# GpSimd's first loads behind the first modulation pieces, and the second round's down matrices ahead of the ranking wait

## The reference

```python
mod = silu(c) @ w_ada[l] + b_ada[l]          # six vectors of 1024: shift1, scale1, gate1, shift2, scale2, gate2
h = x * (1 + scale1) + shift1
y = token_mixer(h, ...)                      # h @ w_in, attention, spatial gating, branches, w_out
x = layer_norm(ALPHA * x + gate1 * y, ...)
h = x * (1 + scale2) + shift2
y = moe_ffn(h, ...)                          # sigmoid scores, top 4 of 8 groups, top 8 of 64 experts, and a shared expert
x = layer_norm(ALPHA * x + gate2 * y, ...)
```

## Time and profile before

| | us |
|---|---|
| three runs | 3248.99, 3258.33, 3268.69 |
| median of the runs | 3258.33 |
| span of the profiled execution | 3257.8 |
| TensorE busy in it | 3010.5 (92%) |
| VectorE busy in it | 1343.3 (41%) |
| layer 0: start and mixer, up to the router | 0 to about 271 |
| layer 0: expert stage | about 271 to 771 |
| layer 1: expert stage | about 1014 to 1516 |

### The profile page before, as it was taken

One profiled execution on the slowest core, in us unless ns is written; L12 is line 12 of the kernel. 1 busy time (PEld: TensorE's weight loads), 2 busy tenths in 40 slices (PEclk: granted clock), 3 DMA queues, 4 the chain that ended last, 5 costly groups with the idle time before them and its releaser, 6 DMA issues.

```text
span 3257.8 us, 65550 instructions
## 1 busy us (share of the span) xinstructions
PE 3010.5 (92%) x28216; PEld 2277.8 (70%) x28216; DVE 1343.3 (41%) x2300; ACT 648.5 (20%) x1253; POOL 173.2 (5%) x160
## 2 busy tenths in 40 slices
PE   7999999888999998887999999999998989998999
PEld 6877555455877665555867744488878877896888
DVE  6645332225545332224553256353057255555100
ACT  0112111111121111112342210000044324442100
POOL 1000000000000000000000000000013201430000
PEclk9999999998999999998998999999999999999999
DMA  9936999999736999997110135374330113001442
GB/s 392 369 149 263 420 420 420 420 421 356 307 117 242 420 420 420 420 420 313 39 65 1 52 131 191 118 281 143 122 104 4 54 38 117 5 4 45 150 152 94
DMA packets 99598, 702.41 MB, mean 216 GB/s; under 512 B 11328, under 2 KB 11504, under 8 KB 16608
## 3 DMA queue, kind: packets, MB, share of 16 engines
q1 hardware_dynamic: 95584, 685.47, 53.4%
q0 software_dynamic: 3712, 12.61, 1.2%
HBM read 696.98 MB, written 1.05 MB: 214 GB/s over the span
## 4 chain that ended last, share of the span: by engine, by line
PE 77%; DMA 12%; DVE 6%; ACT 2%; issue 1%; SPq 1%; POOL 0%; DVEq 0%; ACTq 0%; POOLq 0%
PE ps L229 18%; PE ps L1791 10%; PE ps L1776 10%; PE ps L1314 8%; DMA arena<-in_w_up 6%; DMA arena<-in_w_down 5%; PE ps L2467 5%; PE ps L1342 4%; PE ps L2185 3%; DVE arena L162 3%; PE ps L690 2%; PE ps L1400 2%; PE ps L718 2%; ACT arena L145 2%; PE ps L2482 1%
## 5 line engine op out<-in xcount | busy, mean ns | idle before, releaser
L145 ACT ACTIVATE arena<-ps 128x512 f32<-128x512 f32 (+2 forms) x562 | 284.1, 506 | 1391.7 <-PE ps L1776 298.6
L229 PE MATMUL ps<-arena 128*128 128x256 f32 x2336 | 529.8, 389 | 13.3 <-DVE arena L171 4.7
L229 PEld LDWEIGHTS ps<-arena 128*128 128x128 f32 x2336 | 452.2, 195 | 86.2 <-ACT arena L145 5.7
L1314 PE MATMUL ps<-arena 128*32 128x256 f32 (+2 forms) x5120 | 390.8, 390 | 48.9 <-DMA arena<-in_w_up 47.2
L1314 PEld LDWEIGHTS ps<-arena 128*32 128x32 f32 (+2 forms) x5120 | 249.5, 120 | 194.4 <-issue 104.2
L1776 PE MATMUL ps<-arena 128*128 128x512 f32 (+1 forms) x1024 | 334.0, 487 | 3.5 <-DVE arena L171 3.4
L1791 PE MATMUL ps<-arena 128*128 128x256 f32 x1536 | 333.3, 379 | 0.0
L1791 PEld LDWEIGHTS ps<-arena 128*128 128x128 f32 x1536 | 291.4, 190 | 41.0 <-issue 1.7
L1776 PEld LDWEIGHTS ps<-arena 128*128 128x128 f32 x1024 | 193.3, 190 | 139.3 <-issue 118.4
L1342 PE MATMUL ps<-arena 128*32 128x512 f32 (+2 forms) x1280 | 205.9, 651 | 44.0 <-DMA arena<-in_w_down 43.7
L166 DVE SCALAR_TENSOR_TENSOR arena<-arena,cond 128x1024 f32<-128x1024 f32 x182 | 233.8, 1284 | 28.6 <-DMA arena<-in_w_ada 20.0
(11 more groups left out here) (237 smaller groups left out, 2868.5 us busy)
## 6 DMA issues: line engine op xcount, KB each, us to landing
arena<-in_w_gate SPq DMA_DIRECT2D x128, 1024.0 KB, 19.7
arena<-in_w_up SPq DMA_DIRECT2D x128, 1024.0 KB, 20.0
arena<-in_w_down SPq DMA_DIRECT2D x128, 1024.0 KB, 20.1
arena<-in_mlp SPq DMA_DIRECT2D x80, 1024.0 KB, 4.8
arena<-in_w_ada SPq DMA_DIRECT2D x48, 1024.0 KB, 11.5
arena<-in_ada SPq DMA_DIRECT2D x48, 1024.0 KB, 4.9
arena<-in_w_in SPq DMA_DIRECT2D x30, 1024.0 KB, 10.2
arena<-in_w_rkv SPq DMA_DIRECT2D x20, 1024.0 KB, 4.9
```

What stands on the lines that cost most here:

```text
L145: self.e.activation(out, in_, func, bias=bias, scale=scale, **more).then_inc(*self.done(key))
L229: ins = pe.matmul(out, a, b, start=start and i == 0, stop=stop and i == len(pairs) - 1)
L1314: ins = pe.matmul(psum.of["gu", l, new][o:o_, i_ * 256:i_ * 256 + 256], xe[:, k, new % 2 * 128 + o:new % 2 * 128 + o_], w[i_].rearrange("p ...
```

## The change

GpSimd waits for modulation piece 5 to have landed before it issues the load of x, and for piece 7 before it issues the eleven tables behind it. In the expert stage the down matrices of round 1 are loaded before the wait for `ids`, and no longer between the gate and the up matrices of round 2. They take slots 4 and 5; gate 2 moves to slots 6, 7 and 8; up 2 stays in 9 to 11, and all later loads keep their slots (down 2 is in 3, 4 and 5, as before).

```diff
@@ moe_sp
+            def second_matrices(p):
+                for e in places_of(p):
+                    load(sp, ("w_down", l, e), ("yd", l, p, 1), expert_rows(sp, "w_down", l, e))
+
             for p, new, _, _ in rounds(l):
                 if new == 2:
+                    second_matrices(p)
                     sp.wait_ge(*at["ids", l])
                 if new is not None:
                     for e in places_of(new):
                         load(sp, ("w_gate", l, e), ("gate", l, new), expert_rows(sp, "w_gate", l, e))
-                if p >= 0:
-                    for e in places_of(p):
-                        load(sp, ("w_down", l, e), ("yd", l, p, 1), expert_rows(sp, "w_down", l, e))
+                if p >= 0 and new != 2:
+                    second_matrices(p)
                 if new is not None:
                     for e in places_of(new):
                         load(sp, ("w_up", l, e), ("up", l, new), expert_rows(sp, "w_up", l, e))
@@ pool
             gp.dma_start(tri, D["tri"]).then_inc(*tables["tri"]("tri", 16))
+            gp.wait_ge(*at["mod piece", 5])
             gp.dma_start(XS[:, :].rearrange("p (t n) -> p t n", t=2), D["x"].rearrange("(t p) n -> p t n", p=128)) \
                 .then_inc(*tables["x"]("x", 16))
+            gp.wait_ge(*at["mod piece", 4 * FROM[0] - 1])
             mixer_pool(gp, 0)
             gate_bias(gp, 0, 2)
             gate_bias(gp, 0, 5)
```

## The result

The changed kernel takes 3274.41 us (median of five runs, 3269.02 to 3283.74), the kernel before 3261.3 us in the runs beside it. The ratio is 1.0051, with a 95% interval of 1.0036 to 1.0066: 13.1 us by the medians, 16.6 us by the ratio, which is not the quotient of the medians. The profiled execution took 3269.02 us, with a span of 3267.2; it is the fastest of the five.

A forecast was written before the change was run, and what follows sets the result against it. It took TensorE's chain behind x and modulation piece 7 to bound the start, and DMA the expert stages. Start +14.9 and down matrices +5.8 gave +20.7 us on 3258.33, so 3279 us, range 3260 to 3288.

The forecast's parts named there:

- x starts TensorE's chain, and 24.0 us follow it: At the start, the first product with w_in can begin no earlier than 24.0 us after x lands.
- Piece 5 at 21.9: At the start, modulation piece 5 lands at 21.9 us, and GpSimd issues x then instead of at 2.93.
- x takes 13.3 us: Load of x beside a full SyncE queue: 5.8 us fixed plus 7.5 us for 1 MB, so x lands at 35.2.
- The start costs 14.9 us: First w_in product begins at 59.2 instead of 44.28: +14.9 us, between +6.4 and +16.4, carried through to the end.
- The down matrices cost 2.9 us a layer: Expert stages: shifted slots delay later loads by more than the filled hole saves, +2.9 us per layer, +5.8 for both.
- 2.3 + 0.6 + 1.1 - 5.0: Expert stage: later queue restart 2.3, engines dry 0.6, shorter backlog 1.1, less 5.0 us for bytes moved early.
- 3.85: Expert stage: DMA engines stand 3.85 us because down 2 needs slots 4 and 5, held by down 1.
- The clock gives back nothing: At the start, the granted clock's possible gain on the 112 matmuls, at most 2.0 us, was taken as 0.
- x comes quickly: Rival at the start: x needs only 4.8 us, the start loses 6.4, total +12.2 us, 3270.5; chance 0.12.
- The early down matrices pay in full: Rival in the expert stages: hole filled for nothing, -10.0 us, total +4.9, 3263; chance 0.18.
- the faster case: Rival: expert stages gain the full 10.0 us and x lands before 30.3; with x at 26.7, 3254.7; chance 0.06.

The follow-up runs named there:

- e5: e1 with TensorE's transposes of x moved behind the warming matmuls and the first vector's sums; 3257.62 us, ratio 1.0000 to the kernel before.
- e1: The kernel before plus only GpSimd's two waits, with the old expert stages; 3274.01 us, ratio 1.0046.
- e7: The kernel before with x issued as GpSimd's first instruction, without a wait, and the tables held until modulation piece 7; 3259.72 us, ratio 1.0005.
- e2: The kernel before plus only the down matrices of round 1 loaded ahead of the ranking wait, with the old start; 3259.93 us, ratio 1.0000.
- e10: e7 with the second gate bias, the tables that rope and gating don't need, `ltri` and `tri` held until piece 27; 3250.23 us, ratio 0.9972.
- e8: e7 with only the first gate bias behind piece 7, and `ltri`, `tri` and the other ten tables behind piece 15; 3259.50 us, ratio 0.9996.

## Why the prediction was right, and where it was off

- **x starts TensorE's chain, and 24.0 us follow it.** Right: 23.4 in the changed kernel (57.38 - 33.99), and e5 shows that it is the work in between that counts.
- **Piece 5 at 21.9.** Right: x was issued at 21.94.
- **x takes 13.3 us.** Too long by 1.4: 11.9, and 12.0 to 12.1 in e1, e5 and e7. The fixed part taken from the later table load (5.8 us) was too large, for x's first packet moved after 3.9; the 7.5 us for its bytes came out as 8.0. The whole is still far from the 4.8 us of an idle queue. The Trainium skill's fit ("DMA: Bandwidth & Descriptors", section "Anatomy of one DMA — SWDGE (gpsimd) path"), an estimate of 4.4 us, was not borne out beside a full queue of SyncE: no load of x in these runs took under 11.0 us.
- **The start costs 14.9 us.** 13.1: 1.2 us less since x landed at 33.99 and not at 35.2, 0.6 less since 23.4 us followed it and not 24.0. That nothing of it is given back in the mixer holds (e1).
- **The down matrices cost 2.9 us a layer.** The mechanism and its places are right (restart 2.4 us later, a hole at 342 to 345 where 341.9 to 345.7 follows from my figures and the shift of 12.9). The sum of the term was 2.7 us at down 3 in the first layer and 1.8 in the second, and it shrinks to about 1 us at the end of the second stage; I had carried 2.9 through twice. The traces let the parts be compared, if bytes that the engines did not move are counted at 420 GB/s (an estimate). From 25 us ahead of gate 0 to 20 behind it they moved 339 GB/s before and 348 after in the first layer, 315 and 333 in the second: 1.0 and 1.9 us saved, where 2.3 + 0.6 + 1.1 - 5.0 is 1.0 saved. From 20 to 50 us behind gate 0 it was 419 and then 365, in the second layer 377 after: the later gap costs 3.9 and 3.1 us, where I had 3.85. So the second layer saves more and loses less; why it does was not tried. I also said that TensorE's first wait comes at down 3; it comes at up 3 (1.72 us), which changes nothing behind it.
- **The clock gives back nothing.** Right, but the reason I gave for a possible gain was wrong: TensorE waited 2.80 us ahead of the product, and the granted clock fell there again (0.66 in 56 to 60 us). The 112 matmuls took 26.05 us, before 26.21.
- **The rivals.** "x comes quickly" is out. "The early down matrices pay in full" and with it the faster case are out by e2's trace. The total, 3274.4 us, lies in the range, nearer its middle than its forecast of 3279: 2.7 + 1.8 us instead of 5.8, and 13.1 instead of 14.9. That the total is off by only 4.6 us is in part luck: the median of the kernel before rose by 3.0 us with two more runs. The change itself was forecast at 20.7 us and came out at 16.6 by the ratio, 13.1 by the medians.
- **Not in the prediction:** the volume bound behind the start. It did not matter for this change, which is late, but it decides every version that is early.

## What to carry to other kernels

Before a load is held back to make room for others, count what its first reader has queued behind it: here 21 us of warming work stood behind the transposes of x, and moving the reader (e5) was worth 15 us where moving the load cost 13. In a ring of slots a load that goes out early holds its slot until its use, and the load that needs that slot next waits longer: look at when the slot comes free, not only at the hole that is filled. When an earlier start brings nothing in the end, look for the stretch in which the DMA engines never stand and for the first hole behind it: loads not needed before have to go into that hole (e10); merely later (e8) is not enough.

## What the runs showed that was not expected

One megabyte from GpSimd took 11.0 to 15.1 us at the start in all kernels, wherever it was issued, even ahead of the kernel's other work on GpSimd (e7: 12.0 us).

The time of the kernel before varies by some 20 us over its runs (3248.99 to 3268.69 in the first five), and part of that has one place. In 1710 to 1730, in the attention of the second block, the trace of before has a granted clock of 0.57 (65 matmuls started, above); e2, whose code there is the same, has 0.83 and starts 99:

```profile
1710.00:1730.00 20.00, 20.00 (x99) 14.64 (x99) 6.12 (x12) 4.91 (x11) 0.00 (x0) 0.83 0.00 1
```

From the end of the second expert stage to the end of that attention it takes 322.8 to 323.3 us in ten of the thirteen profiles and 316.7 to 317.5 us in three (e2, e5, e7). What decides between the two is not shown, with one profile a kernel. A single profile's span says little about a change of 5 us; the distance between two matmuls of the changed stage says more.
